# Second model of a two-model kernel: projection, retention, head norm and recurrent inputs as one stage

## The reference

```
h = modulate(rms_norm_2(x, norm1_g), shift1, scale1)
p = h @ w_in                       # 1024 x (2048 retention + 1792 RWKV + 1536 convolution)
q, k, v, g = jnp.split(p_ret, 4, axis=-1)
y_ret  = retention(q, k, v, g, positions, ret_gn_g)   # rotary, two chunks, head norm, silu(g) * out
y_rwkv = rwkv7_time_mix(p_rwkv, ...)                  # token shift, low-rank w, a, g, recurrence
y_conv = short_conv(p_conv, conv_w)                   # b * conv3(c * h)
gates = jax.nn.sigmoid(h @ w_gate + b_gate)
merged = sum over i of gates[i] * (y_i @ w_branch[i])
x = x + gate1 * (merged @ w_o)
x = x + gate2 * hier_moe(modulate(rms_norm_2(x, norm2_g), shift2, scale2))
```

## Time and profile before

| | |
|---|---|
| median of 3 runs | 2702.97 us (2702.05 to 2707.49) |
| profiled execution | 2705.52 us |
| its span | 2703.6 us |
| PE busy | 2125.8 us, 79% of the span |
| DVE, ACT, POOL busy | 638.3, 355.2, 59.5 us |
| TensorE clock granted, mean | 0.891 of full |
| read from HBM | 776.75 MB, 288 GB/s over the span |

### The profile page before, as it was taken

The page is one execution under the profiler, slowest core; times in us unless marked ns, Lnnn a source line. Parts: engine busy times, 40 slices in busy tenths (PEclk is TensorE's granted clock), DMA queues, the critical chain, the costliest instruction groups (busy, mean ns, idle before and its releaser), DMA issues. The chain is left out here.

```text
span 2703.6 us, 33481 instructions
## 1 busy us (share of the span) xinstructions
PE 2125.8 (79%) x14160; PEld 1320.0 (49%) x14161; DVE 638.3 (24%) x1408; ACT 355.2 (13%) x719; POOL 59.5 (2%) x96
## 2 busy tenths in 40 slices
PE   7787779888777997899766666689789987666665
PEld 5564336564336856788422223177577873223222
DVE  4441004541102145454200000012451121000001
ACT  1520000610002013201100000010321020000000
POOL 0200000200000000000000000000010000000000
PEclk9999889989889997899988878799988998888888
DMA  9249999229996430286699999964200438999997
GB/s 386 112 169 428 428 429 389 81 89 385 428 428 265 183 129 2 103 332 259 269 428 428 429 428 429 427 262 156 93 3 32 175 137 359 428 428 429 428 429 309
DMA packets 55840, 779.33 MB, mean 288 GB/s; under 512 B 6840, under 2 KB 7096, under 8 KB 8120
## 3 DMA queue, kind: packets, MB, share of 16 engines
q1 hardware_dynamic: 55736, 777.82, 69.3%
HBM read 776.75 MB, written 1.05 MB: 288 GB/s over the span
## 5 line engine op out<-in xcount | busy, mean ns | idle before, releaser
L1842 PE MATMUL bank<-ring,arena 128*32 128x512 f32 x3136 | 501.5, 776 | 332.9 <-DMA ring<-in_w_exp 328.5
L1842 PEld LDWEIGHTS bank<-ring,arena 128*32 128x32 f32 x3136 | 101.8, 126 | 724.5 <-DMA ring<-in_w_exp 492.6
L1867 PE MATMUL bank<-ring,arena 128*32 128x512 f32 x1568 | 196.5, 639 | 73.2 <-DMA ring<-in_w_exp 50.5
L886 PE MATMUL bank<-xnT,ring 128*128 128x256 f32 x960 | 211.5, 384 | 9.5 <-ACT xnT L369 9.5
L2022 DVE TENSOR_TENSOR arena<-bank,arena 128x256 f32<-128x256 f32 (+1 forms) x33 | 18.3, 554 | 785.6 <-PE bank L1842 558.7
L886 PEld LDWEIGHTS bank<-xnT,ring 128*128 128x128 f32 x960 | 184.7, 193 | 36.8 <-DMA ring<-in_w_conv 5.7
L1573 PE MATMUL bank<-xnT,ring 128*128 128x256 f32 x768 | 178.4, 386 | 10.6 <-PEq L1014 10.6
L1573 PEld LDWEIGHTS bank<-xnT,ring 128*128 128x128 f32 x768 | 149.0, 194 | 33.3 <-issue 12.2
L1812 PE MATMUL bank<-arena 128*128 128x256 f32 x592 | 143.3, 396 | 3.6 <-DVE arena L2033 3.6
L1812 PEld LDWEIGHTS bank<-arena 128*128 128x128 f32 x592 | 113.9, 198 | 60.8 <-issue 46.2
L1867 PEld LDWEIGHTS bank<-ring,arena 128*32 128x32 f32 x1568 | 50.3, 114 | 191.0 <-issue 96.1
(11 more groups left out here) (366 smaller groups left out, 2089.7 us busy)
## 6 DMA issues: line engine op xcount, KB each, us to landing
ring<-in_w_exp SPq DMA_DIRECT2D x288, 2048.0 KB, 25.7
arena<-in_w_ada SPq DMA_DIRECT2D x24, 2048.0 KB, 11.8
ring<-in_w_in SPq DMA_DIRECT2D x20, 2048.0 KB, 20.7
ring<-in_w_merge SPq DMA_DIRECT2D x18, 2048.0 KB, 7.8
ring<-in_w_o SPq DMA_DIRECT2D x8, 2048.0 KB, 10.8
ring<-in_w_conv SPq DMA_DIRECT2D x6, 2048.0 KB, 26.4
ring<-in_w_rest SPq DMA_DIRECT2D x2, 1696.0 KB, 26.5
small<-in_small SPq DMA_DIRECT2D x2, 1440.0 KB
```

What stands on the lines that cost most here:

```text
L886: last = nc.tensor.matmul(o[:, T * j:T * j + T], w[:, k, col:col + P], xnT[:, k, :], start=k == 0, stop=k == KT - 1)
L1842: last = nc.tensor.matmul(o[rows(e), :], Xw[:, k, rows(e)], ring[:, slot(n), at:at + MW], start=k == 0, stop=k == KT - 1)
L1867: last = nc.tensor.matmul(o[rows(e), :], hidT[:, j, rows(e)], ring[:, slot(n), at:at + MW], start=j == 0, stop=j == ft - 1)
```

## The change

The five calls `project2`, `retention`, `head_norm("nret", ...)`, `rwkv_inputs` and `rwkv_turn` become one call of a new `project2` with one block. The groups come in another order: q, k, v, the gate of retention, then the recurrent r, k, v, the low-rank columns, and the convolution last (its h, c, b). The small PE pieces stand between groups. The main lines:

```
-CONV, RWKV, LORA, RET, MERGE, OUT2, MOE2 = 0, 3, 6, 7, 11, 20, 22
+RET, RWKV, LORA, CONV, MERGE, OUT2, MOE2 = 0, 4, 7, 8, 11, 20, 22
...
-            return [(dram["w_conv2"][l, n], SLOT) for n in range(3)] + [(dram["w_in2"][l, n + 4], SLOT) for n in range(3)]
+            return [(dram["w_in2"][l, n], SLOT) for n in range(RING)]
...
+            Q, V, GATE, R, K_, V_, LOW, CONV_H, CONV_C, CONV_B = 0, 4, 6, 8, 10, 12, 14, 15, 17, 19
...
+                    def group(i):
+                        n = groups[i][0]
+                        o = bank[i % 4]
...
+                        if i >= 4:
+                            pe.wait_ge(taken, i - 3)
...
+                    def key_sums():
+                        pe.wait_ge(flat_ready, 2)
+                        pe.wait_ge(kk_sq, 1)
...
+                    def turn_tokens():
+                        pe.wait_ge(g_ready, 2)
+                        pe.wait_ge(q_ready, 1)
+                        pe.wait_ge(bonus_ready, 2)
...
+                    for i in range(len(groups)):
+                        group(i)
+                        if i == V + 1:
+                            turn_retention()
+                        if i == GATE:
+                            score_retention()
+                        if i == GATE + 1:
+                            out_retention()
+                        if i == R:
+                            means()
+                        if i == R + 1:
+                            variances()
+                        if i == V_ + 1:
+                            key_sums()
+                        if i == CONV_H:
+                            pe.wait_ge(log_ready, 2)
+                            pe.wait_ge(ms_ready, 2)
+                            pe.wait_ge(low_ready, 2)
+                            lora(0)
+                            lora(1)
+                        if i == CONV_H + 1:
+                            pe.wait_ge(w_ready, MT)
+                            lora(2)
+                        if i == CONV_C + 1:
+                            bonus_sums()
+                        if i == CONV_B:
+                            turn_tokens()
...
+                    for i in range(K_, V_ + 2):
+                        take(i)
+                    act.wait_ge(kk_ready, 1)
+                    nc.scalar.activation(sq, khT, ACT.Square).then_inc(kk_sq, 1)
+                    take(LOW)
+                    for i in range(2):
+                        act.wait_ge(ms_ready, i + 1)
+                        nc.scalar.activation(sq[:, 2 * i:2 * i + 2, :], sq[:, 2 * i:2 * i + 2, :], ACT.Ln).then_inc(kk_log, 1)
+                    act.wait_ge(kk_log, 2)
+                    nc.scalar.activation(sq, sq, ACT.Exp, scale=-0.5).then_inc(kn_ready, 1)
+                    nc.scalar.preload_act_table(ACT.Sigmoid)
+                    act.wait_ge(low_shifted, 1)
+                    nc.scalar.activation(lowT[0:64, 0, :], lowT[0:64, 0, :], ACT.Tanh).then_inc(low_ready, 1)
+                    nc.scalar.activation(lowT[:, 1, :], lowT[:, 1, :], ACT.Sigmoid).then_inc(low_ready, 1)
+                    take(CONV_H)
...
                 project2(l)
-                retention(l)
-                head_norm("nret", y_ret, ar(13824, MT, T), "ones", P, HEPS, V2("ret_gn_g_2"), gated(y_ret, sgT))
-                rwkv_inputs()
-                rwkv_turn()
                 rwkv_solve()
```

## The result

The changed kernel takes **2643.14 us** (median of 4 runs, 2638.2 to 2648.29) against 2703.94 us before (4 runs, 2702.05 to 2707.49). The ratio is **0.977**, 95% interval 0.9755 to 0.9785: 60.8 us less. The forecast was 2641 us.

A forecast was written before the change was run, and what follows sets the result against it. Behind PE-bound groups, a chain of short hand-overs between engines was the bound. Each layer swaps 55.25 and 54.74 us for 21.3 + 1.7 + 1.05 = 24.05, saving 61.9 us: 2641 us predicted, range 2634 to 2660.

The forecast's parts named there:

- one block end: Between the stage's last matmul and the solve's first transpose: the only block end that remains, 1.05 us in each layer.
- The added PE work: Small pieces placed between PE's groups: transposes, 128- and 512-column matmuls and low-rank products add 21.3 us in each layer.
- the price of 0.216 us for each instruction: Low-rank products on PE: 24 instructions of 256 columns, priced from the merge stage, 5.2 us in all.
- Rival 1: Small pieces between groups cost what they did alone: gain falls by 9.6 + 9.0 us, 2660 us; 0.17 including small seam losses.
- One stall: Ahead of the key sums behind group 13: PE waits 1.7 us for ACT's last v copy and squares of k.
- The slack at `lora(0)`: Low-rank activations on ACT take 5.2 us under group 15's 6.87 us: hidden with 1.7 us to spare.
- All other steps: Turning, scores, output, means, variances, the long DVE chain and the bonus product: their waits are hidden under groups.
- rival 2: ACT becomes the bound around key sums and low-rank products: some 9 us more, 2650 us; chance 0.05.
- rival 3: Clock falls to its lower level inside the merged stage; with half of it slow, 2809 us; chance 0.02.
- The rule of the Trainium skill: Going round PSUM banks leaves gaps that move the clock; half the stage might run at 1.2 GHz, ending in a loss.
- The 2.4 GHz level "throughout": PE in the new stage: full clock assumed all through, since its longest idle time would be 1.7 us.
- a warmer clock in the solve: At the start of the solve: some us gained, not counted in the sum, included only in the range's lower end.

The follow-up runs named there:

- `groups_first`: Changed kernel, still one stage, but PE does all 21 groups first and every small piece behind them; 2706.65 us against 2706.64 before, ratio 1.0001.
- `low_late2`: Changed kernel with three useless ACT passes of 1024 columns ahead of the low-rank activations; PE waits 1.30 us there in both layers, second layer's stage 1.34 us longer.
- `filled_in_waits`: Kernel before the change with useless 512-column matmuls sized to end inside PE's waits, keeping the clock up; 2690.94 us against 2705.36, ratio 0.9951.
- `in_a_row`: Changed kernel with the five pieces of retention and its mean and variance in a row behind group 9, no group between; 2652.46 us, ratio to before 0.9799.
- `square_early`: Changed kernel with ACT's squares of k moved ahead of the copy of the last v group; 2638.99 us, ratio to before 0.9752.

## Why the prediction was right

**The bound.** The prediction read 55.25 and 54.74 us behind the last group as a chain of hand-overs with no engine busy, and let them go but for one block end. `groups_first` gives all of it back by the order alone, so the gain is not in having one stage as such. One reading was slightly off: in the earlier trace rows the loads end with a slice of 0.8 from 995 to 1001.75 us, so the queue is idle from about 1002 and not 995 us. Nothing hangs on it.

**The added PE work.** The forecast was 21.3 us in each layer. By start-to-start times of the after trace the pieces are 1.74 (transposes of q, k) + 3.12 (to the scores) + 2.68 (output) + 1.71 + 1.71 + 1.79 (means, variances, key sums) + 2.89 + 1.73 (low-rank) + 1.72 (bonus) + 1.74 (last transposes) = 20.8 us. Each is within 0.1 us of its price but for the first low-rank products, 0.6 us cheaper: the price of 0.216 us for each instruction came from products over all 128 rows, and these use 64. Rival 1, pieces as dear as on their own, is refuted: no seam shows a loss of more than 0.1 us.

**The waits.** One stall was named and priced at 1.7 us; the trace has 1.72, charged to the ACT squares, but taking it away gives 1.96, so the term was 0.26 us short. The slack at `lora(0)` was put at 1.7 us and is 1.9 (`low_late2`). All other steps were hidden as walked through, and rival 2 did not come about.

**The clock.** Its mean was 0.99, and 1.00 behind the first 6 us of the stage, so rival 3 fell. The rule of the Trainium skill ("TensorE: Matmul & The Clock Gate", "A second HAM failure mode: psum-queue depth-cycling") did not apply to this stage. The 2.4 GHz level "throughout" was not quite right: the first six groups took 43.81 and 42.97 us to the next start, where 41.20 were the price at the full clock. The stage before also started low, and its 146.7 us hold that, so only the difference counts. What the clock is worth in the old stretch was part of the sum without a figure; `filled_in_waits` puts it at 5 to 6 us of each 30. Some us from a warmer clock in the solve, named for the lower end of the range, did not come.

**The sum.** 61.9 us were forecast and the stages gave 61.4: 30.4 for 31.2 and 30.9 for 30.7. The pieces were 0.5 us cheaper each time, the stall 0.26 us dearer, and the first layer's groups some 0.9 us slower to get going. That the sum comes within 0.5 us owes something to these misses pointing both ways. The forecast of the median, 2641 us, is 2 us low, inside the spread of the runs (2638 to 2648).

## What to carry to other kernels

Where one stage keeps an engine full and the next is a chain of short hand-overs, weave the chain's pieces between the first stage's groups: the pieces then cost their start-to-start time and nothing for the hand-over. It is the order that pays: one stage with the pieces behind all groups gave 0 us here. The single stage is needed, since a piece can only stand between groups of its own stage. Walk through the new order with one group as the unit, look for pieces whose input is queued behind the copy of the group just ahead of them, and put that work one copy earlier.

## What the runs showed of the hardware

Most of the time that POOL worked, DVE stood still. In the changed kernel four small products of the convolution (L1239) take 4.45 us, while POOL runs its two products. `pool_later` holds POOL back until DVE has passed the convolution.

> The changed kernel with POOL's two products held back until DVE has done the convolution. In the changed kernel four DVE products of the convolution take 4.45 us while POOL works, and the like took 1.14 us where POOL was idle. Theory (POOL holds DVE up while both work): they take about 1.1 us here. Rival (the form or the place of the operands in memory makes them slow): 4.4 us again. The stage is as long either way, since the last group covers both.

Measured: in the changed kernel, DVE and POOL:

```profile
1002.46 4.45 DVE L1239 TENSOR_SCALAR arena<-small,vec 128x256 f32<-128x256 f32 x4
1002.63 1.95 POOL L1135 TENSOR_TENSOR arena<-arena,pc 128x1024 f32<-128x1024 f32 x1 [431.51 <-DVE arena L1237]
1004.54 1.95 POOL L1137 TENSOR_TENSOR arena<-arena,pc 128x1024 f32<-128x1024 f32 x1
```

and with POOL later:

```profile
1000.54 1.13 DVE L1240 TENSOR_SCALAR arena<-small,vec 128x256 f32<-128x256 f32 x4
```

1.13 us in place of 4.45: DVE lost 3.3 us beside 3.9 us of POOL. It lost them in two lumps and not in shares: of the four DVE products two take 2.00 us each, one beside each product of POOL (1.95 us), and the other two 0.34 us, as without POOL. The stage is as long as it was (171.55 and 170.72 us), since the last group covers both; the single time of that kernel, 2648.12 us, is within the changed kernel's spread. The Trainium skill ("SBUF — State Buffer", "Who interferes with whom") calls the port pair that the two engines share an exclusive lock: while an instruction of one of them that needs it holds it, the other fully blocks. The trace agrees, with 2.00 us for a product of 0.34; whether these DVE products ran in a mode that needs both ports no trace here tells.

The two 64-row products already ran faster than their columns say when issued four and four (2.89 us for 16 instructions, 0.18 us each, against 0.216 for the full-height form), and in turn they took 1.93 us, 0.12 us each, so products on different rows of the array must overlap.

A wait on PE can cost some 0.25 us more than its idle time shows, most of it the tail of the last matmul ahead of it. It came out in `in_a_row` (4.47 us lost for 3.46 us of brackets) and in `square_early` (1.96 for 1.72), but not in `low_late2` (1.34 for 1.30).
